# Turned gate product, an earlier sum in the matrix memory, two early output products, and waits moved in the feed-forward blocks

## The reference

```
dt = softplus(dt_raw + dt_bias);  lf = log_sigmoid(gates + fg_bias)   # [tokens, 2 x (16 + 8 + 8)]
```

## Time and profile before

| what | us |
|---|---|
| median of 3 runs (lowest, highest) | 3392.99 (3392.69, 3396.45) |
| the profiled execution | 3392.56 |
| its span in the trace | 3390.8 |
| PE matmul busy | 3250.4 (96%) |
| DVE, ACT, POOL busy | 1680.9, 1031.9, 1123.7 |

### The profile page before, as it was taken

How to read it: one execution, slowest core, us unless ns; L and a number is a source line. 1 busy time by engine, 2 the same in 40 slices (tenths; PEclk the granted TensorE clock), 3 DMA queues, 4 the chain that set the end, 5 groups by cost and what they waited for, 6 DMA issues and landing times.

```text
span 3390.8 us, 51552 instructions
## 1 busy us (share of the span) xinstructions
PE 3250.4 (96%) x16950; PEld 2632.0 (78%) x16950; DVE 1680.9 (50%) x2837; ACT 1031.9 (30%) x2083; POOL 1123.7 (33%) x908
## 2 busy tenths in 40 slices
PE   9999999999999999998999999989999899799997
PEld 7787888867776788886546888868888588688886
DVE  3454545555555445644446554445453534354544
ACT  3433323123332332213316343123221334222311
POOL 0023445323221344441001433435444231444443
PEclk9999999999999999997999999989999899899999
DMA  3222222221111122221210211212222111122222
GB/s 121 80 85 95 81 91 76 81 81 63 50 57 50 58 91 81 93 75 57 68 56 20 69 56 56 81 68 81 93 80 94 55 65 63 50 81 93 80 93 75
DMA packets 68670, 249.36 MB, mean 74 GB/s; under 512 B 7568, under 2 KB 7568, under 8 KB 68544
## 3 DMA queue, kind: packets, MB, share of 16 engines
q1 hardware_dynamic: 68544, 247.72, 21.7%
HBM read 245.59 MB, written 2.10 MB: 73 GB/s over the span
## 4 chain that ended last, share of the span: by engine, by line
PE 86%; DVE 5%; issue 5%; ACT 2%; POOL 1%; DMA 1%; DVEq 0%; POOLq 0%; ACTq 0%; SPq 0%
PE psum L2210 55%; PE psum L2145 10%; PE psum L439 6%; PE psum L1764 3%; PE psum L1351 1%; PE psum L1789 1%; PE psum L2313 1%; PE psum L471 1%; PE psum L509 1%; DVE residual L2671 1%; DVE stream L2669 1%; ACT scratch L1056 1%; DMA w_ring<-units 1%; PE psum L493 1%; DVE stream L2613 1%
## 5 line engine op out<-in xcount | busy, mean ns | idle before, releaser
L2210 PE MATMUL psum<-scratch 128*128 128x256 f32 (+1 forms) x3600 | 815.0, 383 | 9.6 <-ACT scratch L2379 6.3
L2210 PEld LDWEIGHTS psum<-scratch 128*128 128x128 f32 x3600 | 683.3, 190 | 117.0 <-ACT scratch L2379 8.7
L2844 POOL TENSOR_TENSOR scratch<-w_ring 128x512 f32<-128x512 f32 (+2 forms) x160 | 203.7, 1273 | 1360.5 <-DMA w_ring<-units 767.7
L2379 ACT ACTIVATE scratch<-psum 128x264 f32<-128x264 f32 (+1 forms) x480 | 185.0, 387 | 884.0 <-PE psum L2210 845.0
L2694 DVE TENSOR_TENSOR scratch<-scratch,psum 128x264 f32<-128x264 f32 (+1 forms) x264 | 108.4, 424 | 501.2 <-PE psum L2210 473.3
L2210 PE MATMUL psum<-scratch,w_ring 128*128 128x256 f32 (+1 forms) x1200 | 275.6, 382 | 0.0
L2210 PEld LDWEIGHTS psum<-scratch,w_ring 128*128 128x128 f32 x1200 | 227.9, 190 | 34.9
L2210 PE MATMUL psum<-acts,w_ring 128*128 128x264 f32 (+1 forms) x1088 | 246.8, 385 | 2.6 <-ACT scratch L2494 1.1
L2210 PEld LDWEIGHTS psum<-acts,w_ring 128*128 128x128 f32 x1088 | 207.3, 191 | 35.5 <-issue 2.5
L2442 ACT ACTIVATE scratch<-scratch,params 128x528 f32<-128x528 f32 (+1 forms) x176 | 144.4, 821 | 274.8 <-DVE scratch L2694 274.8
L2848 POOL TENSOR_TENSOR scratch<-scratch,w_ring 128x512 f32<-128x512 f32 (+2 forms) x160 | 221.0, 1381 | 12.8
(11 more groups left out here) (454 smaller groups left out, 4712.1 us busy)
## 6 DMA issues: line engine op xcount, KB each, us to landing
w_ring<-units SPq DMA_DIRECT2D x463, 512.0 KB, 3.6
residual<-x_t SPq DMA_DIRECT2D x4, 528.0 KB, 6.1
out_t<-residual SPq DMA_DIRECT2D x4, 512.0 KB, 2.7
params<-cols SPq DMA_DIRECT2D x1, 568.5 KB, 8.1
gate_w_sb<-gate_w SPq DMA_DIRECT2D x1, 96.0 KB, 10.0
```

Of the source, the lines that this page charges most:

```text
L2210: mm = nc.tensor.matmul(out, weights(k), moving(k), start=(p in (1, 2, 5) and k == 0), stop=(k == h - 1), skip_group_check=(p != 2))
L2379: nc.scalar.activation(kept(q, n, H), quad_bank(q, p, H), ACT.Copy).then_inc(q_copied, 1)
L2844: g.tensor_tensor(s(1), row(1, 0), row(1, 1), ALU.add).then_inc(q_weight, 1)
```

## The change

- The gate product is turned: the 64 gate columns (one 128 x 64 weight tile per k) become the stationary operand, 256 tokens the moving one, k is the outer loop, and the two token halves go to PSUM partitions 0 to 63 and 64 to 127. ACT copies this to `mx_rows`; after the next tile, PE transposes it back in four pieces (`turn_gates`) into banks 2 and 3, and ACT copies those to `mx_raw`. Only this second copy frees the bank of tile 0. Three semaphores are merged into `mx_turned`.
- In mLSTM heads 1 to 7, DVE does `add_vo(i, 2)` after the fourth of the 8 scaled arguments and not after the eighth.
- The products (1,0) and (1,1) of the first body of `fox_out` are issued in the attention's last pair, at its steps 0 and 3. For this, products 1, 6, 7, 4 of `fox_out` use banks 6 and 7. The two bodies of `fox_out` are written out instead of looped, on PE and ACT.
- In `ffn` on ACT the pad wait comes after the first copies of p = 1, and the copies of p = 1 of the first `down` body come before the last `gelu`.

```
-        def quad_bank(q, p, H):
+        def quad_bank(q, p, H, b=None):
+            if b == BODIES["fox_out"] and BANK_OF[p] == 0:
+                return PS[:, 6 + q, 0:H]
             return PS[:, 3 * q + BANK_OF[p], 0:H]
...
                 if m // NS + 1 < KD:
                     piece(m // NS + 1, m % NS)
+                elif m % NS in (0, 3):
+                    if m % NS == 0:
+                        pe.wait_ge(fx_values, KD)
+                        pe.wait_ge(S("fx_out"), 5 * KD // 2 + 1)
+                    quads(0, BODIES["fox_out"], UNITS["fox_out"], KD // 2, T1, CHUNKS["fox_out"], lambda k, t, e: A[:, k, t:e],
+                          products=(PRODUCTS[m % NS // 3],))
...
-            for j in range(NC4):
-                for k in range(KD):
-                    if j == 0:
-                        pe.wait_ge(*when("mixin", "x", k + 1))
-                    mm = nc.tensor.matmul(PS[:, TILES["ssd_pre"] % 2, 64 * j:64 * j + 64], h(k)[:, P * j:P * j + P], W[:, s, k, 0:64],
-                                          start=(k == 0), stop=(k == KD - 1))
...
+            for k in range(KD):
+                pe.wait_ge(*when("mixin", "x", k + 1))
+                for q in range(2):
+                    mm = nc.tensor.matmul(PS[64 * q:64 * q + 64, TILES["ssd_pre"] % 2, 0:2 * P], W[:, s, k, 0:64], h(k)[:, 2 * P * q:2 * P * q + 2 * P],
+                                          start=(k == 0), stop=(k == KD - 1), skip_group_check=True)
...
+            def turn_gates():
+                pe.wait_ge(S("mx_rows"), 1)
+                for j in (0, 2, 1, 3):
+                    r = slice(64 * (j // 2), 64 * (j // 2) + 64)
+                    mm = nc.tensor.transpose(PS[:, 2 + j // 2, 64 * (j % 2):64 * (j % 2) + 64], mx_rows[r, P * (j % 2):P * (j % 2) + P], ID[r, r])
+                mm.then_inc(S("mx_turned"), 1)
...
             for t in range(3):
                 tile("ssd_pre", 1 + t)
+                if t == 0:
+                    turn_gates()
...
-            a.activation(mx_raw, PS[:, TILES["ssd_pre"] % 2, 0:256], ACT.Copy).then_inc(tile_free, 1)
+            a.activation(mx_rows, PS[:, TILES["ssd_pre"] % 2, 0:256], ACT.Copy).then_inc(S("mx_rows"), 1)
+            act.wait_ge(S("mx_turned"), 1)
+            a.activation(mx_raw.rearrange("p (b c) -> p b c", b=2), PS[:, 2:4, 0:P], ACT.Copy).then_inc(tile_free, 1)
...
+                    if q == 4 and not first:
+                        add_vo(i, 2)
                     v.tensor_scalar(ml_d[:, d, j, lo:hi], PS[:, 2 + d, lo:hi],
...
-                else:
-                    add_vo(i, 2)
...
+                    if name == "fox_out":
+                        quads(0, b, u0, count // 2, T, chunk, moving, products=PRODUCTS[2:])
+                        quads(1, b, u0, count // 2, T, chunk, moving)
+                        continue
...
+                    if name in FFNS and c == 0:
+                        body(0, b, (2, 3))
+                        body(1, b)
+                        continue
...
-                act.wait_ge(*when(name, "pad", 1))
...
                 copies(0, b, T, (1,))
+                act.wait_ge(*when(name, "pad", 1))
...
                 convolved(NF // 2 - 1)
+                copies(0, b + NF // 2, T, (1,))
                 gelu(NF // 2 - 1)
```

More of the change, by code:

```diff
@@ L393, in fox_scores_at, with fox_pe @@
             return 512 * (4 + (n % 2 if n < 8 else 0))
-        def fox_pe(pe, unit, buffer_free, gemm, gemm_tokens, h):
+        def fox_pe(pe, unit, buffer_free, gemm, gemm_tokens, h, quads):
             def product(i, q, p):
@@ L807, in ssd_pe @@
             s = unit(UNITS["ssd_pre"], 0, 0, 0)
[L808 to L816 removed]
+            for k in range(KD):
[3 more added lines that the diff above has]
+                                          start=(k == 0), stop=(k == KD - 1), skip_group_check=True)
+                if k == 0:
+                    mm.then_inc(w_started, 1)
+            mm.then_inc(tile_full, 1)
+            def turn_gates():
[4 more added lines that the diff above has]
+                mm.then_inc(S("mx_turned"), 1)
             def tile(name, t):
@@ L2336, in _ @@
             norm("ffn0", T1, True)
-            fox_pe(pe, unit, buffer_free, gemm, gemm_tokens, x1)
+            fox_pe(pe, unit, buffer_free, gemm, gemm_tokens, x1, quads)
             projection("fox_out", T1)
@@ L2378, in copies, with body @@
                         act.wait_ge(q_added, add_done(i, b, what, q, before=1))
-                        nc.scalar.activation(kept(q, n, H), quad_bank(q, p, H), ACT.Copy).then_inc(q_copied, 1)
+                        nc.scalar.activation(kept(q, n, H), quad_bank(q, p, H, b), ACT.Copy).then_inc(q_copied, 1)
             def down(name, b, T):
                 H = T // 2
-                def body(i, b):
-                    copies(i, b, T)
+                def body(i, b, states=(1, 2, 3)):
+                    copies(i, b, T, states)
                     for q in range(2):
@@ L2387, in body @@
                         act.wait_ge(q_added, add_done(i, b, "12", q, before=1))
-                        nc.scalar.activation(kept(q, 4, H), quad_bank(q, 4, H), ACT.Copy).then_inc(q_copied, 1)
+                        nc.scalar.activation(kept(q, 4, H), quad_bank(q, 4, H, b), ACT.Copy).then_inc(q_copied, 1)
                 for c in range(len(KS[name])):
+                    if name in FFNS and c == 0:
+                        body(0, b, (2, 3))
+                        body(1, b)
+                        continue
                     if name == "mix_out" and c == 0:
@@ L2393, in down @@
                         mlstm_out(act, 8)
+                        body(1, b)
+                        continue
+                    if name == "fox_out":
+                        body(0, b)
                         body(1, b)
```

17 lines of the change are left out of this document (8 added, 9 removed).

## The result

The changed kernel takes 3364.76 us (median of 4 runs, 3361.96 to 3366.74), the kernel before beside it 3394.5 us (4 runs, 3392.69 to 3396.45): a ratio of 0.9913, 95% interval 0.9897 to 0.9928. The prediction was 3366.7, its range 3361 to 3377. The span of the profiled execution goes from 3390.8 to 3363.5 us, 27.3 less; the prediction booked 26.3.

The account below looks back on a forecast made before the run. PE was taken as the bound, busy 96% of the span. Gains of 9.0 + 7.6 + 3.4 + 3.0 + 3.3 = 26.3 us off 3392.56 gave 3366.3, with 0.4 for the median 3366.7; range 3361 to 3377.

Parts of the forecast that it names:

- Gate product: Mixer entry: turned product falls from 15.24 to 6.5 us; with the tile behind and turn costs, 9.0 us gain booked.
- Rival 3: Mixer entry: idle moment before the third tile drops the clock for one 3.4 us stretch, 1.7 us more, 3368.4; chance 0.05.
- The chain behind it: Mixer entry, ACT's copy to the last time steps: starts one tile later, 10.0 us long, with 4 us of cover.
- Second sum: mLSTM heads: wait before `values_gate` 5 goes, 0.4 us returns before scores 2; 7.6 us gained over seven heads.
- Rival 2: mLSTM: scores 2 or ACT's copy holds PE instead; gain 2 instead of 7.6 us, 3372.3; chance 0.10.
- Early products: Last attention pair: two output products, 3.7 us together, move into idle time; 3.4 us gained, bounds 2.0 and 4.6.
- Pad wait and early copies: Feed-forward: waits at the third and fourth starts go, 3.0 us; waits at four down-product starts go, 3.3 us.
- Rivals 1 and 4: 1: clock stays low in new gate product, 3369 or 3376, 0.13; 4: clock falls in mLSTM loop, 3400, 0.02.
- rival 1: Mixer entry: clock does not rise during the new gate product; 3369, or 3376 without overlap of the halves; chance 0.13.
- the best case of the gate product: Mixer entry: upper bound of the gate product's gain, 10.0 us, with the clock up after 4.5 us.

## Why the prediction was right, step by step

- **Gate product.** Booked 8.7 for the product, 1.5 for the tile behind it, -1.1 for turn and wait. Measured 10.0, 1.5, and -0.9 (0.34 of transposes, 0.48 of idle, the rest between them). The product's term was too small since the clock rose 3.2 us after its start and not 5.7: the first feed-forward was the wrong row to take the rise from. What then ends the product is the delivery of the tiles of h, a bound that the prediction read (last tile at 1588.84, 4.46 us after the start) and did not use. Over the nine other traces of this form it rose after 2.9 to 5.2 us and the product took 5.1 to 6.2; the booked 6.5 is just above them all. What the sum lacked is the low stretch behind the sums, about 1.7 us. Rival 3 had one in kind, from the idle time before the third tile, but it stands 17 us behind that idle time, and the experiments do not show the one to be its cause. The two misses cancel, 8.8 for 9.0, and that is luck.
- **The chain behind it.** Nothing came late: PE has no other new bracket up to the first broadcast. 4 us of cover were enough.
- **Second sum.** The mechanism is as written, with the new wait before scores 2 that was forecast at 0.4 and is 0.44. 7.1 for 7.6 (the prediction's own terms, two of 1.0 and five of 1.1, add up to 7.5): 9.1 less 2.0, which is the new bracket in five heads (0.26, then four times 0.44). The two heads with the shortest waits show no new one, as forecast. Rival 2 (the wait renamed, 2 us) falls.
- **Early products.** Both are hidden. 3.1 us of output products for the 3.4 booked. The 1.0 booked for the second one's delay and the 0.7 for the clock cannot be told apart in the pair's end, which did not move; that the products hold the clock up is not shown.
- **Pad wait and early copies.** 6.3 booked, 7.2 measured, of which by the brackets: third block 1.27 + 1.06 less the new 0.43, fourth 1.73 + 1.00. The forecast said that PE has no new wait at the down products; it has this one, since DVE's sum there is now the later. With 0.27 us for each bracket one gets 6.3 for the six that went, less 0.43 for the new one, and five times 0.27 more, 7.2. That it meets the measured 7.2 so well is luck: the same blocks differ by 3 us in sum from trace to trace. The direction is firmer, since the kernel before lies 6.3 to 9.5 us above all eleven.
- **Rivals 1 and 4.** The clock rose in the new product in all ten traces of it, and the mLSTM loop stayed at 1.00. The experiment with the old product shows how near rival 1 lay: in that form the clock does not come back while PE is fully busy.

The Trainium skill ("TensorE: Matmul & The Clock Gate", A second HAM failure mode: psum-queue depth-cycling) names short idles between groups as a cause of falls. The runs bear it out in part: the falls at 1578.4 and at 1582.0 in the two traces above stand behind 3.40 us in which PE was busy for 1.11 and 0.96, and that at 1059.9 before behind one with 0.42. But the new bracket of 0.48 us did not bring a fall at its place in any of eight traces, and that the old product stayed at 0.50 with PE busy throughout is not covered by that section.

Two smaller slips changed nothing: the best case of the gate product adds up to 9.7 and not 10.0, and the chances of the cases beyond 0.2% to 0.95 and not 0.94. In sum the prediction lies 1.9 us above the median. Three of its terms are too high, by 0.2, 0.5 and 0.5 us, one too low by 0.9, and 1.3 us came from stages that it did not book. The executions of the changed kernel spread by 10 us over two sessions, so that nearness is in part luck; the terms by stage are the better test.

## What to carry to other kernels

Put the narrow matrix on the stationary side and stream the tokens: it halves the records and here let the clock rise, and two 64-column halves side by side took another 40% off, down to what DVE's delivery allows; the turn back costs 0.3 us plus one evacuation, if the bank is given back by the first copy. When a wait in a fixed rhythm is removed, work out at once which wait stands next and by how much it is late; here the sum gave 0.4 us where 0.44 was measured, and pointed to the next edit, worth 3.9 us. Price an edit of a few us by anchors in the trace of its own stage, not by the median of the whole kernel.

## What the runs showed of the hardware

- Matmuls of 64 columns behind 128-column weight loads: the clock stayed at 0.50 with PE busy for 14.60 of 14.60 us (it had fallen behind 3.40 us in which PE was busy for 0.96); in 256-column records of the same product it rose 2.9 to 5.2 us after the start, in ten traces.
- 32 records of 256 columns in two halves of the array took 5.1 to 6.2 us, partly at half clock; 16 records of 512 columns in one half took 8.6. The 5.1 is where DVE delivers the last operand (4.46 us after the start).
- A change between full tiles and 64-row or 64-column work moved the next record back by some 0.1 us (0.52 for 0.43 us, 0.33 for 0.22).
- Low stretches of 3.4 us move: over the fourteen traces one stands behind the sums in six, in the last attention pair in six, at 1801 to 1810 in four, and in the linear attention (2856 to 2883) in seven, whatever part was edited. One costs up to 1.7 us (half of its 3.4). That they are why executions of one kernel spread by up to 10 us is likely (the changed kernel's two traces differ by such stretches), but the unprofiled executions have no trace.
- A wait cost PE some 0.27 us more than its bracket in the mLSTM heads (0.7 us per head for 0.44), since the overlap of two neighbouring records goes with it and the record behind it is longer.
